# The first convolution pair: both column groups on each quarter of the tokens, and a first half loaded as two quarters

## The chip, the cores and the metric

The kernel is one program on one core of a Trainium2 chip. The metric is the device time of that core in microseconds (us), the median of the runs. On this kernel a difference of about 0.2%, some 3.8 us, is what a measurement can tell from no change.

## What is computed

One layer of a hybrid decoder. Tokens are 16 meta tokens, 256 prompt tokens and 8 sequences of 8 new tokens, 336 in all, each with 2048 features. Cut to the lines that concern the start:

```python
xn = rmsnorm(x, g_mix)                       # 336 tokens x 2048
z = xn @ w_in + b_in
zq, zk, zv, zi, zf, zo, zu, zc, zb, zga, zgb = jnp.split(z, _split_points(), axis=-1)
...
conv_out, conv_state = conv_fn(zc * zu, w_conv)   # 1024 channels, 3 taps, causal
y_b = zb * conv_out
```

All is in float32. The mLSTM heads, the gated merge and the squared-ReLU MLP follow and are not touched by the change.

## The kernel before

**Products and units.** Every float32 operand is split into a high and a low part, and a product is three matmuls (high by high, high by low, low by high; line 1250 issues each). The weights come in units of 512 rows by 256 columns (512 KB). One unit is 24 matmuls: 4 blocks of 128 rows, 2 blocks of 128 columns, 3 products. A unit passes through a ring of four slots on its way: SP loads it into `raw` (L378), ACT copies its high part (`w_high`, L543), DVE subtracts to get its low part (`w_low`, L823), and PE multiplies. Semaphores tie the four: SP refills a slot once its low part is made, ACT and DVE write a slot's parts once PE has used the unit that was in it. So each engine works through the units in one fixed order, written out in its own program.

**The start.** The tokens arrive token by token in `x_tok`, in two halves of 1024 feature columns: five DMAs each, on SP's queue (`tokens`, L364 to L373). PE transposes them, two blocks of 128 columns at a time (six transposes, L1270), into one of two pairs of PSUM banks, `XBANKS`. From there ACT makes `x_high` (L561), scaled by a column of `vec_T`, DVE makes `x_low` (L840) and a plain copy `x_T` (L843). `vec_T` itself comes from four small DMAs on ACT's queue (`vec_rows`), a transpose on PE (L1258) and a copy on DVE (L816). ACT also sums the squares of the tokens (L551), from which DVE and ACT make the norm's factors; PE spreads them over the partitions (`scales`, `r_diag`), and DVE copies the result to `r_bc` (L871).

**The first convolution pair.** For 256 channels, the columns of zu and then those of zc are computed, four units each: numbered here 0 to 3 (zu, accumulated in `ACC[0]`) and 4 to 7 (zc, `ACC[1]`). The first units are interleaved with the transposes: unit 0 needs the first quarter of the features, and so on. DVE takes each group out of PSUM and multiplies it by `r_bc` (`tmp`, L900), ACT adds the bias (L588, L594), and DVE multiplies zu by zc and runs the three taps (L904 to L925). The other three pairs follow, units 8 to 15 being the second; two of the pairs are a loop. On ACT and DVE a unit's split stands ahead of its use by three (`LEAD`), so before the taps of pair 0 DVE has made the low parts through unit 10.

Of the kernel before, what the change touches and what calls it, by code (L numbers as in the profile page):

```python
# [29 lines left out]
P = 128  # L30
# [13 lines left out]
def build(nc, x_prompt, x_sample, state_C, state_n, state_m, state_conv, meta, g_mix, w_in, b_in,  # L44
# [65 lines left out]
    with ExitStack() as ctx:  # L110
# [121 lines left out]
        HEAD_ACC = [0, 1, 0, 1, 2]  # L232
        XBANKS = [ACC[1], ACC[2]]

# [13 lines left out]
        s_brows = sem("bias_rows_in")  # L248
        s_xtok = [sem(f"x_tok_in{n}") for n in range(6)]
        s_gw = sem("gate_w_in")  # L250
# [112 lines left out]
        def _(sp):  # L363
            def tokens(half):  # L364

                c = slice(D // 2 * half, D // 2 * half + D // 2)
                in0, in1, in2 = s_xtok[3 * half:3 * half + 3]
# [12 lines left out]

            def convolution(i, extra=()):
                for g, col in enumerate((CU, CC)):
                    for u in range(NU):
                        if NU * g + u in extra:
                            extra[NU * g + u]()
                        stream(UCV * i, NU * g + u, win, u, col + GC * i)

            def small():
# [139 lines left out]
        def _(act):  # L528
# [16 lines left out]
            def sum_squares(half, n):  # L545

                nt, done = (P, P, NMETA + TS)[n], 3 * half + n
                act.wait_ge(s_xtok[done], 16 if n == 1 else 32)
# [24 lines left out]
            def gate_weights():  # L573
# [4 lines left out]
                a.activation(gws[:, :, 32:32 + H], gw[:, :, H:2 * H], ACT.Copy).then_inc(s_ghl, 1)  # L578

            def convolution(i, extra=()):  # L580
                for p in range(UCV):
                    split(UCV * i, p + LEAD)
                    if p in extra:
                        extra[p]()
                    if p == 3:
                        act.wait_ge(evacuated, 2 + 2 * i + 1)
                        for b in range(GB):
                            ins = a.activation(zu[:, b, :], tmp[:, b, 0:TZ], ACT.Identity,  # L588
                                               bias=biasT[:, ds(BU + GB * i + b, 1)])
                        ins.then_inc(s_zu, 1)  # L590
                    if p == 7:
                        act.wait_ge(evacuated, 2 + 2 * i + 2)
                        for b in range(GB):
                            ins = a.activation(tmp[:, b, 0:TZ], tmp[:, b, 0:TZ], ACT.Identity,  # L594
                                               bias=biasT[:, ds(BC_ + GB * i + b, 1)])
                        ins.then_inc(s_zc, 1)

# [15 lines left out]

            convolution(0, {1: root, 2: gate_weights, 3: lambda: act.wait_ge(s_col, 2)})
            with act.Fori(1, H - 1) as i:
# [192 lines left out]
        def _(dve):  # L808
# [29 lines left out]
            for k in range(KB):  # L838
# [3 lines left out]
                if k % 2 == 1:  # L842
                    v.tensor_copy(xT[:, k - 1:k + 1, T0:T], XBANKS[k // 2 % 2][:, :, T0:T]).then_inc(s_xT, 1)  # L843
                if k % 4 == 3 and k // 4 < LEAD:
                    split(0, k // 4)

# [38 lines left out]
            scale_o = rbc[:, T0:T].unsqueeze(1).to_broadcast([P, GB, TO])  # L885

            def convolution(i, extra=()):
                for p in range(UCV):
# [3 lines left out]
                    if p in (3, 7):  # L892
                        g = p // 4
                        dve.wait_ge(unit_used, RING + UCV * i + 4 * g + 4)
                        if g == 0:
                            dve.wait_ge(s_z, 1 + i)
                            dve.wait_ge(s_cv, 1 + 12 * i)
                        else:
                            dve.wait_ge(s_zu, i + 1)
                        v.tensor_tensor(tmp[:, :, 0:TZ], ACC[g][:, :, 0:TZ], scale_z, ALU.mult).then_inc(evacuated, 1)  # L900
                    if p == 7:

                        dve.wait_ge(s_zc, i + 1)
                        v.tensor_copy(zs[:, :, :, 0:TAPS - 1], stT[:, ds(GB * i, GB), :, :])  # L904
                        v.tensor_tensor(zp[:], tmp[:, :, 0:ZP], zu[:, :, 0:ZP], ALU.mult)
                        v.tensor_tensor(zs[:, :, :, TAPS - 1:], tmp[:, :, ZP:TZ].rearrange("p g (b t) -> p g b t", t=DS),
                                        zu[:, :, ZP:TZ].rearrange("p g (b t) -> p g b t", t=DS), ALU.mult) \
                            .then_inc(s_z, 1)
                        dve.wait_ge(s_z, 1 + i + 1)
                        v.tensor_copy(zlast[:, ds(GB * i, GB), 0:TAPS - 1], zp[:, :, ZP - TAPS + 1:ZP])  # L910
                        v.tensor_copy(zlast[:, ds(GB * i, GB), TAPS - 1:].rearrange("p g (b r) -> p g b r", r=TAPS - 1),
                                      zs[:, :, :, DS:DS + TAPS - 1])

                        for r in range(TAPS):
                            for b in range(GB):
                                w = vecT[:, ds(VC + r * (CW // P) + GB * i + b, 1)]
                                out_p = yb[:, ds(GB * i + b, 1), 0:SEQ]
                                out_s = yb[:, ds(GB * i + b, 1), SEQ:TO].rearrange("p o (b t) -> p (o b) t", t=DS)
                                src_p = zp[:, b:b + 1, r:r + SEQ]
                                src_s = zs[:, b, :, r:r + DS]  # L920
                                for out, src in ((out_p, src_p), (out_s, src_s)):
                                    if r == 0:
                                        v.tensor_scalar(out, src, w, None, ALU.mult).then_inc(s_cv, 1)
                                    else:
                                        v.scalar_tensor_tensor(out, src, w, out, ALU.mult, ALU.add).then_inc(s_cv, 1)  # L925
                            dve.wait_ge(s_cv, 1 + 12 * i + 4 * r + 4)


# [53 lines left out]

            convolution(0, {1: columns, 3: scales, 5: gate_weights})
            with dve.Fori(1, H - 1) as i:
# [263 lines left out]
        def _(pe):  # L1248
# [11 lines left out]
            def tokens(k):  # L1260

                for n in range(3):
                    pe.wait_ge(s_xtok[3 * (k // (KB // 4)) + n], 16 if n == 1 else 32)
                if k >= 2:
# [48 lines left out]

            def convolution(i, extra=()):
                for p in range(UCV):
                    if p in extra:
                        for work in extra[p]:
                            work()
# [4 lines left out]
            def four_blocks(u):  # L1323

                return [lambda: tokens(2 * u), lambda: tokens(2 * u + 1), lambda: pe.wait_ge(s_xl, UK * u)]

            tokens(0)
            tokens(1)
            convolution(0, {0: four_blocks(1), 1: four_blocks(2), 2: four_blocks(3) + [columns],
                            3: [lambda: pe.wait_ge(s_xl, KB)], 4: [scales]})  # L1330
            with pe.Fori(1, H - 1) as i:
# [230 lines left out]
```

## Time and the profile before

| | |
|---|---|
| runs | 1911.57 us median of 3 (1911.06 to 1912.3) |
| profiled execution, first to last instruction | 1911.0 us |
| PE busy | 1889.9 us (99%) |
| DVE busy, ACT busy | 941.6 us (49%), 689.5 us (36%) |

The page gives no time of the profiled execution but its span; the median of the runs is 0.57 us above it. PE is busy nearly all the time, so what can be gained or lost is time in which PE waits, or runs at its low clock.

### The profile page before, as it was taken

To read this page: it belongs to the slowest core of one execution; us is meant where nothing else is said; L and a number is where in the kernel's file an instruction comes from. 1 tells how busy PE (TensorE), PEld (TensorE's weight loads), DVE (VectorE), ACT (ScalarE), POOL (GpSimd) and SP (SyncE) were. 2 spreads that over 40 slices of the span, in tenths; PEclk is the share of its full clock that TensorE was granted. 3 is DMA by queue.
4 is the path that set the end of the run, shared out by engine and by line. 5 is a ranking of instruction groups with operands and counts; after the bars stand their busy time and mean duration, and the time that the engine had idled before them with its cause. 6 is when DMAs were issued, how large, how long until landed. Compare 5 with 4: busy or idle time off the path is not lost.

```text
span 1911.0 us, 33610 instructions
## 1 busy us (share of the span) xinstructions
PE 1889.9 (99%) x12647; PEld 1855.8 (97%) x12647; DVE 941.6 (49%) x1045; ACT 689.5 (36%) x825; POOL 34.5 (2%) x67
## 2 busy tenths in 40 slices
PE   7999999999999999999999999999999999999998
PEld 7999898989899999999999999999999999999997
DVE  6565545454454444445555544455444544455544
ACT  5344343434343333333443333333333333333331
POOL 1001000010100000000000000000000000000000
PEclk9999999999999999999999999999999999999998
DMA  7446564756465545544454444444444444444442
GB/s 208 144 127 190 132 213 133 220 119 216 138 177 146 151 143 155 152 148 148 143 172 156 140 159 145 151 150 141 160 145 151 150 147 154 143 154 151 145 155 78
DMA packets 294469, 293.86 MB, mean 154 GB/s; under 512 B 12506, under 2 KB 292314, under 8 KB 294300
## 3 DMA queue, kind: packets, MB, share of 16 engines
q1 hardware_dynamic: 283464, 282.67, 48.8%
q10 hardware_dynamic: 10692, 9.51, 1.6%
q0 software_dynamic: 272, 1.12, 0.1%
q8 instruction: 27, 0.44, 0.1%
q14 instruction: 14, 0.11, 0.0%
HBM read 281.10 MB, written 12.17 MB: 153 GB/s over the span
## 4 chain that ended last, share of the span: by engine, by line
PE 98%; DVE 1%; DMA 0%; issue 0%; ACT 0%; SPq 0%; DVEq 0%; ACTq 0%
PE ps L1250 97%; DVE y_out L1243 0%; PE ps L1350 0%; DMA x_tok<-in_x_sample_dram 0%; PE ps L1270 0%; DVE x_low L840 0%; DVE x_T L843 0%; PE ps L1507 0%; DVE w_low L823 0%; ACT x_high L561 0%; PE ps L1451 0%; DVE sq_acc L1216 0%; DVE x_T L1212 0%; ACT tmp L790 0%; DVEq L110 0%
## 5 line engine op out<-in xcount | busy, mean ns | idle before, releaser
L823 DVE TENSOR_TENSOR w_low<-raw,w_high 128x1024 fp32r<-128x1024 f32 x512 | 621.7, 1226 | 609.0 <-ACT w_high L543 605.1
L543 ACT ACTIVATE w_high<-raw 128x1024 fp32r<-128x1024 f32 x512 | 534.9, 1055 | 712.5 <-PE ps L1250 709.1
L1250 PE MATMUL ps<-x_high,w_high 128*128 128x320 f32 (+2 forms) x2432 | 755.5, 311 | 1.3 <-PE ps L1250 1.1
L1250 PE MATMUL ps<-x_low,w_high 128*128 128x320 f32 (+2 forms) x2432 | 755.8, 311 | 0.0
L1250 PE MATMUL ps<-x_high,w_low 128*128 128x320 f32 (+2 forms) x2432 | 753.2, 310 | 0.0
L1250 PEld LDWEIGHTS ps<-x_high,w_high 128*128 128x128 f32 x2432 | 457.5, 188 | 7.2 <-issue 4.6
L1250 PEld LDWEIGHTS ps<-x_high,w_low 128*128 128x128 f32 x2432 | 458.6, 189 | 0.0
L1250 PEld LDWEIGHTS ps<-x_low,w_high 128*128 128x128 f32 x2432 | 457.3, 188 | 0.1
L1250 PE MATMUL ps<-u_high,w_high 128*128 128x320 f32 x1024 | 316.5, 309 | 0.0
L1250 PE MATMUL ps<-u_low,w_high 128*128 128x320 f32 x1024 | 316.4, 309 | 0.0
L1250 PE MATMUL ps<-u_high,w_low 128*128 128x320 f32 x1024 | 316.4, 309 | 0.0
L1250 PEld LDWEIGHTS ps<-u_high,w_high 128*128 128x128 f32 x1024 | 192.2, 188 | 0.0
L1250 PEld LDWEIGHTS ps<-u_low,w_high 128*128 128x128 f32 x1024 | 192.2, 188 | 0.0
L1250 PEld LDWEIGHTS ps<-u_high,w_low 128*128 128x128 f32 x1024 | 192.2, 188 | 0.0
L1250 PE MATMUL ps<-merged_high,w_high 128*128 128x320 f32 x256 | 79.1, 309 | 0.0
L1250 PE MATMUL ps<-merged_low,w_high 128*128 128x320 f32 x256 | 79.1, 309 | 0.0
L1250 PE MATMUL ps<-merged_high,w_low 128*128 128x320 f32 x256 | 79.1, 309 | 0.0
L774 ACT ACTIVATE u_high<-u_squared 128x640 f32 (+1 forms) x32 | 23.7, 739 | 140.2 <-DVE u_squared L1191 140.2
L1212 DVE TENSOR_TENSOR x_T<-ps,x_T 128x640 f32 (+1 forms) x32 | 26.4, 825 | 54.1 <-PE ps L1250 54.1
L1250 PEld LDWEIGHTS ps<-merged_high,w_high 128*128 128x128 f32 x256 | 48.0, 188 | 0.0
L1250 PEld LDWEIGHTS ps<-merged_low,w_high 128*128 128x128 f32 x256 | 48.0, 188 | 0.0
L1250 PEld LDWEIGHTS ps<-merged_high,w_low 128*128 128x128 f32 x256 | 48.0, 188 | 0.0
(250 smaller groups left out, 1160.2 us busy)
## 6 DMA issues: line engine op xcount, KB each, us to landing
raw<-in_w_in_dram SPq DMA_DIRECT2D x176, 512.0 KB, 3.8
raw<-in_w_up_dram SPq DMA_DIRECT2D x128, 512.0 KB, 3.9
raw<-in_w_down_dram SPq DMA_DIRECT2D x128, 512.0 KB, 3.4
raw<-in_w_o_dram SPq DMA_DIRECT2D x32, 512.0 KB, 3.5
C_state<-in_state_mlstm_C_dram SPq DMA_DIRECT2D x16, 512.0 KB, 6.5
raw<-in_state_mlstm_C_dram SPq DMA_DIRECT2D x16, 512.0 KB, 4.1
out_dram<-C_state ACTq DMA_DIRECT2D x8, 1024.0 KB, 6.8
raw<-in_p_a_dram SPq DMA_DIRECT2D x16, 512.0 KB, 4.3
```

Source lines behind the costliest of these rows:

```text
L543: a.activation(wh[:, s % RING], raw[:, s % RING], ACT.Copy).then_inc(high_done, 1)
L774: a.activation(uh[:, ds(GB * j, GB), :], uq[:], ACT.Copy).then_inc(s_uh, 1)
L823: v.tensor_tensor(wl[:, s % RING], raw[:, s % RING], wh[:, s % RING].bitcast(F32), ALU.subtract).then_inc(low_done, 1)
L1212: v.tensor_tensor(x2, ACC[pair][:, :, 0:TO], x2, ALU.add).then_inc(evacuated, 1)
L1250: return pe.matmul(out, lhsT, rhs, start=start, stop=stop)
```

## The change

Three things, all ahead of the second pair. The first half of the tokens' columns comes as two quarters, so there are three parts (`XPARTS`) and fifteen DMAs in place of ten. The first pair's units go by quarter: unit numbers 0, 2, 4, 6 are zu and 1, 3, 5, 7 are zc, and the two that share a quarter follow each other. And the bank pair `ACC[1]`, which now holds zc from the start, is no longer used for transposes; banks 4 and 5 are, where `vec_rows` and the other small rows are transposed too, so PE waits for DVE's copy of `vec_T` before the first token transposes. The later steps of the first pair are written out again for each engine.

The parts, and SP's order of issue (`tokens` takes the part's number, `first_convolution` replaces the first call of the loop's body):

```diff
-        XBANKS = [ACC[1], ACC[2]]
+        XBANKS = [ps[:, 4:6, :], ACC[2]]
+        XPARTS = [(0, D // 4), (D // 4, D // 2), (D // 2, D)]
...
+            def first_convolution(extra):
+                for u in range(NU):
+                    for g, col in enumerate((CU, CC)):
+                        stream(0, 2 * u + g, win, u, col)
+                        if 2 * u + g in extra:
+                            extra[2 * u + g]()
...
             tokens(0)
-            convolution(0, {1: lambda: tokens(1), 3: small, 4: gates})
+            first_convolution({1: lambda: tokens(1), 2: lambda: tokens(2), 3: small, 4: gates})
```

ACT, from the first tokens to the end of the first pair:

```diff
             act.wait_ge(s_set, 1)
-            for n in range(2):
-                sum_squares(0, n)
             act.wait_ge(s_col, 1)
             for k in range(KB):
...
-                if k % 4 == 3 and k // 4 < LEAD:
-                    split(0, k // 4)
-                    if k < 4:
-                        sum_squares(0, 2)
-                    sum_squares(1, k // 4)
+                if k % UK == UK - 1:
+                    u = k // UK
+                    split(0, 2 * u)
+                    split(0, 2 * u + 1)
+                    if u > 0:
+                        for done in (2 * u - 2, 2 * u - 1):
+                            sum_squares(done // 3, done % 3)
...
+            def first_convolution():
+                root()
+                gate_weights()
+                split(0, UCV)
+                act.wait_ge(s_col, 2)
+                bias_u(0)
+                split(0, UCV + 1)
+                bias_c(0)
+                split(0, UCV + 2)
```

DVE behind the splits of the first pair, and PE:

```diff
+            def first_convolution():
+                columns()
+                gate_weights()
+                scales()
+                split(0, UCV)
+                evacuate_z(0, 0, UCV - 1)
+                split(0, UCV + 1)
+                evacuate_z(0, 1, UCV)
+                split(0, UCV + 2)
+                convolve(0)
...
+            def first_convolution():
+                pe.wait_ge(s_col, 1)
+                tokens(0)
+                tokens(1)
+                for u in range(NU):
+                    if u < NU - 1:
+                        tokens(2 * u + 2)
+                        tokens(2 * u + 3)
+                    pe.wait_ge(s_xl, UK * (u + 1))
+                    for g in range(2):
+                        if (u, g) == (NU - 1, 0):
+                            pe.wait_ge(s_xT, KB // 2)
+                            columns()
+                        if (u, g) == (NU - 1, 1):
+                            scales()
+                        if u == 0:
+                            pe.wait_ge(evacuated, g + 1)
+                        unit(0, 2 * u + g, ACC[g][:, :, 0:TZ], xh, xl, UK * u, TZ0, u == 0, u == NU - 1)
```

`evacuate_z`, `convolve`, `bias_u` and `bias_c` are the bodies that stood in the loop before, unchanged. On SP, `gates` (the gate weights' DMA and three tiny ones) now stands behind the load of unit 4 instead of ahead of it.

How the order moves, at three places. ACT at the very start, before (`y_b` is scratch space for the squares, `x_tok_in0` is the landing of the first half's first rows):

```order
L551 ACT_TABLE_LOAD [waits x_tok_in0]
L551 ACTIVATE y_b,sum_sq_halves<-x_tok 128x1024 [waits columns_set]
L551 ACTIVATE y_b,sum_sq_halves<-x_tok 128x1024 [waits sum_sq_ready,x_tok_in1]
L561 ACTIVATE x_high<-ps,vec_T 128x336 [waits x_transposed,cols_ready]
L561 ACTIVATE x_high<-ps,vec_T 128x336 [waits x_transposed] x3
L543 ACTIVATE w_high<-raw 128x1024 [waits unit_used,raw_landed0]
```

and after, the same place:

```order
L567 ACT_TABLE_LOAD [waits x_transposed,cols_ready]
L567 ACTIVATE x_high<-ps,vec_T 128x336 [waits columns_set]
L567 ACTIVATE x_high<-ps,vec_T 128x336 [waits x_transposed] x3
L551 ACTIVATE w_high<-raw 128x1024 [waits unit_used,raw_landed0]
L551 ACTIVATE w_high<-raw 128x1024 [waits unit_used,raw_landed1]
L567 ACTIVATE x_high<-ps,vec_T 128x336 [waits x_transposed] x4
```

The two sums of squares that stood ahead of `x_high` are gone from there, so the load of ACT's function table, which stands ahead of the first activation, now waits for the first transposes (`x_transposed`) and not for the first tokens. Two weight splits follow where one did.

DVE around the end of the first pair, before (`raw_landed` 3, 0, 1, 2 mark the low parts of units 7, 8, 9 and 10; `tmp` is the evacuation of zu, then of zc; `z_sample` begins the product and the taps):

```order
L871 COPY r_bc<-ps 128x336 [waits r_bc_product]
L900 TENSOR_TENSOR tmp<-ps,r_bc 128x2x322 [waits z_ready,conv_step,unit_used,r_bc_ready]
L823 TENSOR_TENSOR w_low<-raw,w_high 128x1024 [waits unit_used,raw_landed3,high_done]
L823 TENSOR_TENSOR w_low<-raw,w_high 128x1024 [waits unit_used,raw_landed0,high_done]
L878 TENSOR_TENSOR gate_w_split<-gate_w,gate_w_split 128x16x4 [waits gate_w_split,gate_w_in]
L880 TENSOR_TENSOR gate_w_split<-gate_w,gate_w_split 128x16x4
L823 TENSOR_TENSOR w_low<-raw,w_high 128x1024 [waits unit_used,raw_landed1,high_done]
L823 TENSOR_TENSOR w_low<-raw,w_high 128x1024 [waits unit_used,raw_landed2,high_done]
L900 TENSOR_TENSOR tmp<-ps,r_bc 128x2x322 [waits zu_ready,unit_used]
L904 COPY z_sample<-conv_state_T 128x16x2 [waits zc_ready]
```

and after (`raw_landed` 0, 1, 2 are units 8, 9 and 10):

```order
L896 COPY r_bc<-ps 128x336 [waits r_bc_product]
L847 TENSOR_TENSOR w_low<-raw,w_high 128x1024 [waits raw_landed0,unit_used,high_done,r_bc_ready]
L919 TENSOR_TENSOR tmp<-ps,r_bc 128x2x322 [waits conv_step,z_ready,unit_used]
L847 TENSOR_TENSOR w_low<-raw,w_high 128x1024 [waits unit_used,raw_landed1,high_done]
L919 TENSOR_TENSOR tmp<-ps,r_bc 128x2x322 [waits zu_ready,unit_used]
L847 TENSOR_TENSOR w_low<-raw,w_high 128x1024 [waits unit_used,raw_landed2,high_done]
L923 COPY z_sample<-conv_state_T 128x16x2 [waits zc_ready]
L924 TENSOR_TENSOR z_prompt<-tmp,zu 128x516
```

Both evacuations now stand between the copy of `r_bc` and the taps, with the low parts of units 8, 9 and 10 put between them one by one. In both kernels the low part of unit 11 is DVE's next piece of work behind the taps.

ACT at the same place, before (`gate_w_split` ends the gate weights; `zu` and `tmp` are the two biases; `raw_landed` 2, 3, 0, 1, 2 are the high parts of units 6 to 10):

```order
L543 ACTIVATE w_high<-raw 128x1024 [waits unit_used,raw_landed2]
L588 ACTIVATE zu<-tmp,bias_T 128x322 [waits evacuated,cols_ready]
L588 ACTIVATE zu<-tmp,bias_T 128x322
L543 ACTIVATE w_high<-raw 128x1024 [waits unit_used,raw_landed3]
L543 ACTIVATE w_high<-raw 128x1024 [waits unit_used,raw_landed0]
L543 ACTIVATE w_high<-raw 128x1024 [waits unit_used,raw_landed1]
L543 ACTIVATE w_high<-raw 128x1024 [waits unit_used,raw_landed2]
L594 ACTIVATE tmp<-tmp,bias_T 128x322 [waits evacuated]
L594 ACTIVATE tmp<-tmp,bias_T 128x322
```

and after (units 8, 9 and 10):

```order
L551 ACTIVATE w_high<-raw 128x1024 [waits unit_used,raw_landed0]
L591 ACTIVATE zu<-tmp,bias_T 128x322 [waits evacuated,cols_ready]
L591 ACTIVATE zu<-tmp,bias_T 128x322
L551 ACTIVATE w_high<-raw 128x1024 [waits unit_used,raw_landed1]
L598 ACTIVATE tmp<-tmp,bias_T 128x322 [waits evacuated]
L598 ACTIVATE tmp<-tmp,bias_T 128x322
L551 ACTIVATE w_high<-raw 128x1024 [waits unit_used,raw_landed2]
```

The high parts of units 9 and 10 now each stand behind a bias, and each bias waits for an evacuation by DVE (`evacuated`).

## Rows read from the trace of the kernel before

**Rows 1.** Page, parts 1 and 6: engines' share; a weight unit's transfer, median to landing.
```profile
PE 1889.9 (99%) x12647; PEld 1855.8 (97%) x12647; DVE 941.6 (49%) x1045; ACT 689.5 (36%) x825; POOL 34.5 (2%) x67
...
raw<-in_w_in_dram SPq DMA_DIRECT2D x176, 512.0 KB, 3.8
```

**Rows 2.** Chain that ended last, in order of time: start us, us, what.
```profile
2.68 6.62 DMA x_tok<-in_x_sample_dram
...
16.41 5.31 PE ps L1250 x24
...
36.22 93.85 PE ps L1250 x631
```

**Rows 3.** Timeline of PE: start us, us, what, idle before and its releaser.
```profile
8.18 0.35 PE L1258 MATMUL ps<-ident,vec_rows 72*128 72x72 f32 x1 [8.18 <-DMA vec_rows<-in_w_conv_dram]
9.44 2.47 PE L1270 MATMUL ps<-ident,x_tok 128*128 128x128 f32 x12 [0.90 <-DMA x_tok<-in_x_sample_dram]
13.38 1.35 PE L1270 MATMUL ps<-ident,x_tok 128*128 128x128 f32 x6 [1.47 <-DVE x_T L843]
...
32.42 0.39 PE L1250 MATMUL ps<-x_high,w_high 128*128 128x322 f32 x1 [0.20 <-DVE w_low L823]
...
36.22 0.89 PE L1250 MATMUL ps<-r_diag,ones 128*128 128x128 f32 x6
36.91 0.39 PE L1250 MATMUL ps<-x_high,w_high 128*128 128x322 f32 x1
```

**Rows 4.** Timeline of ACT over the start, its DMA issues included.
```profile
2.48 0.65 ACTq L538 DMA_DIRECT2D vec_rows<-in_w_conv_dram  x1
5.42 1.28 ACT L551 ACT_TABLE_LOAD   x1 [5.42 <-DMA x_tok<-in_x_prompt_dram]
...
10.89 2.03 ACT L561 ACTIVATE x_high<-ps,vec_T 128x336 fp32r<-128x336 f32 x4 [1.78 <-PE ps L1270]
...
39.81 1.02 ACT L588 ACTIVATE zu<-tmp,bias_T 128x322 f32<-128x322 f32 x2 [3.21 <-DVE tmp L900]
...
52.29 1.02 ACT L594 ACTIVATE tmp<-tmp,bias_T 128x322 f32<-128x322 f32 x2 [3.30 <-DVE tmp L900]
53.21 1.05 ACT L543 ACTIVATE w_high<-raw 128x1024 fp32r<-128x1024 f32 x1
```

**Rows 5.** Timeline of DVE over the start.
```profile
8.57 0.23 DVE L816 COPY vec_T<-ps 128x72 f32<-128x72 f32 x1 [6.32 <-PE ps L1258]
...
38.35 0.50 DVE L871 COPY r_bc<-ps 128x336 f32<-128x336 f32 x1
38.88 0.83 DVE L900 TENSOR_TENSOR tmp<-ps,r_bc 128x644 f32<-128x644 f32 x1
41.81 2.36 DVE L823 TENSOR_TENSOR w_low<-raw,w_high 128x1024 fp32r<-128x1024 f32 x2 [2.10 <-ACT w_high L543]
...
53.34 0.18 DVE L904 COPY z_sample<-conv_state_T 128x32 f32<-128x32 f32 x1 [1.09 <-ACT tmp L594]
...
58.47 3.50 DVE L823 TENSOR_TENSOR w_low<-raw,w_high 128x1024 fp32r<-128x1024 f32 x3 [0.40 <-DVE y_b L925]
```

**Rows 6.** Timeline of SP's queue, 0 to 110 us.
```profile
13.66 7.17 SPq L397 DMA_DIRECT2D ig_bias<-in_b_in_dram  x1
```

**Rows 7.** The x_tok issue of 4.53 us alone: instruction, then issue to landing.
```profile
L369 SPq DMA_DIRECT2D x_tok<-in_x_prompt_dram x1: 449/449/449, 4.5 to 4.5; - x1
...
DMA to landing us min/median/max: 8.4/8.4/8.4
```

**Rows 8.** The raw issue of 8.21 us alone: instruction, then issue to landing.
```profile
L378 SPq DMA_DIRECT2D raw<-in_w_in_dram x1: 680/680/680, 8.2 to 8.2; - x1
...
DMA to landing us min/median/max: 11.1/11.1/11.1
```

**Rows 9.** Timeline of PE at the end of the program.
```profile
1897.19 1.18 PE L1250 MATMUL ps<-ones,sq_acc 128*128 128x1 f32 x6 [2.20 <-DVE sq_acc L1230]
```

**Rows 10.** Windows at the end: stretch, busy time (PE first), granted clock, DMA share, GB/s.
```profile
1897.40:1904.20 6.80, 6.37 (x31) 5.41 (x31) 5.35 (x14) 0.20 (x1) 0.00 (x0) 0.50 0.42 137
```

More of the change, by code:

```diff
@@ L248, in build @@
         s_brows = sem("bias_rows_in")
-        s_xtok = [sem(f"x_tok_in{n}") for n in range(6)]
+        s_xtok = [sem(f"x_tok_in{n}") for n in range(3 * len(XPARTS))]
         s_gw = sem("gate_w_in")
@@ L363, in _, with tokens @@
         def _(sp):
-            def tokens(half):
-                c = slice(D // 2 * half, D // 2 * half + D // 2)
-                in0, in1, in2 = s_xtok[3 * half:3 * half + 3]
+            def tokens(part):
+                c = slice(*XPARTS[part])
+                in0, in1, in2 = s_xtok[3 * part:3 * part + 3]
                 sp.dma_start(xtok[0:NMETA, 0, c], meta[:, c]).then_inc(in0, 16)
@@ L547, in sum_squares @@
                 nt, done = (P, P, NMETA + TS)[n], 3 * half + n
-                act.wait_ge(s_xtok[done], 16 if n == 1 else 32)
+                for part in ((0, 1), (2,))[half]:
+                    act.wait_ge(s_xtok[3 * part + n], 16 if n == 1 else 32)
                 if done > 0:
@@ L578, in gate_weights, with bias_u, bias_c @@
                 a.activation(gws[:, :, 32:32 + H], gw[:, :, H:2 * H], ACT.Copy).then_inc(s_ghl, 1)
+            def bias_u(i):
+                act.wait_ge(evacuated, 2 + 2 * i + 1)
+                for b in range(GB):
+                    ins = a.activation(zu[:, b, :], tmp[:, b, 0:TZ], ACT.Identity,
+                                       bias=biasT[:, ds(BU + GB * i + b, 1)])
+                ins.then_inc(s_zu, 1)
+            def bias_c(i):
+                act.wait_ge(evacuated, 2 + 2 * i + 2)
+                for b in range(GB):
+                    ins = a.activation(tmp[:, b, 0:TZ], tmp[:, b, 0:TZ], ACT.Identity,
+                                       bias=biasT[:, ds(BC_ + GB * i + b, 1)])
+                ins.then_inc(s_zc, 1)
             def convolution(i, extra=()):
@@ L585, in convolution @@
                     if p == 3:
[L586 to L590, printed above, removed]
-                    if p == 7:
[L592 to L596, printed above, removed]
+                        bias_u(i)
+                    if p == 7:
+                        bias_c(i)
+            def first_convolution():
[7 more added lines that the diff above has]
+                split(0, UCV + 2)
             def log1p_exp():
@@ L843, in _ @@
                     v.tensor_copy(xT[:, k - 1:k + 1, T0:T], XBANKS[k // 2 % 2][:, :, T0:T]).then_inc(s_xT, 1)
-                if k % 4 == 3 and k // 4 < LEAD:
-                    split(0, k // 4)
+                if k % UK == UK - 1:
+                    split(0, 2 * (k // UK))
+                    split(0, 2 * (k // UK) + 1)
             def columns():
@@ L892, in convolution @@
                     if p in (3, 7):
[L893 to L900, printed above, removed]
@@ L901, in convolution @@
-                    if p == 7:
[L903 to L926, printed above, removed]
@@ L929, in _ @@
+                        evacuate_z(i, p // 4, p + 1)
+                    if p == 7:
+                        convolve(i)
+            def first_convolution():
[8 more added lines that the diff above has]
+                convolve(0)
             step = [0]
@@ L981, in decays @@
                                   [:, :, DS - 1]))
-            convolution(0, {1: columns, 3: scales, 5: gate_weights})
+            first_convolution()
             with dve.Fori(1, H - 1) as i:
@@ L1260, in tokens @@
             def tokens(k):
+                part = next(i for i, (c0, c1) in enumerate(XPARTS) if c0 <= 2 * P * k < c1)
                 for n in range(3):
-                    pe.wait_ge(s_xtok[3 * (k // (KB // 4)) + n], 16 if n == 1 else 32)
+                    pe.wait_ge(s_xtok[3 * part + n], 16 if n == 1 else 32)
                 if k >= 2:
@@ L1312, in unit, with convolution @@
                 ins.then_inc(unit_used, 1)
-            def convolution(i, extra=()):
+            def convolution(i):
                 for p in range(UCV):
-                    if p in extra:
-                        for work in extra[p]:
-                            work()
                     if p % 4 == 0:
@@ L1321, in convolution @@
                     unit(UCV * i, p, ACC[p // 4][:, :, 0:TZ], xh, xl, UK * (p % 4), TZ0, p % 4 == 0, p % 4 == 3)
[L1323 to L1330, printed above, removed]
+            def first_convolution():
[16 more added lines that the diff above has]
+                        unit(0, 2 * u + g, ACC[g][:, :, 0:TZ], xh, xl, UK * u, TZ0, u == 0, u == NU - 1)
+            first_convolution()
             with pe.Fori(1, H - 1) as i:
```

38 lines of the change are left out of this document (34 added, 4 removed).

## The prediction

> **What bounds the kernel now.** I read the page's first part first. PE is busy 99% of the span [rows 1], so a change to the start can only move the time by what it does to PE's waits and to PE's clock. Then I read the chain that ended last, in order of time: until 9.30 us it is the last tokens of the first half that land, then it goes over PE, ACT and DVE to the first unit at 16.41, and from 36.22 on PE alone carries it [rows 2]. So two things count: when unit 0 starts, and whether PE waits anywhere after it. PE's timeline shows the only such wait of the stretch, 0.20 us at unit 3 for a low part [rows 3]. A unit at full speed takes 24 matmuls at 93.85 / 631 = 0.149 us, 3.57 us; the first one takes 5.31 [rows 2], so it runs mostly at the low level of the clock and loses 1.74 us to it.
>
> The profiled execution has 1911.0 us from first to last instruction. The sum below is made against that; the runs' median lies 0.57 us above it, and I carry that over.
>
> **The start, up to unit 0.** The matmuls, transposes and splits are the same in number before and after; only order and transfers change.
>
> Less data before the first transposes. The first half is 336 rows of 4 KB, 1.38 MB, and its last piece lands at 2.68 + 6.62 = 9.30 [rows 2]. Its first two pieces (0.52 MB) had landed by 5.42, when ACT's wait for them ended [rows 4]. A first quarter has 0.69 MB. Between these two points that gives 6.2 us.
>
> `vec_rows`, which PE now also has to wait for, landed at 8.18 [rows 3]. Its last issue, at 2.48 [rows 4], stands between the pieces of the first half, and it landed before the piece issued at 2.68 did; transfers of the two queues seem to be served nearly in order of issue. With half the bytes ahead of it, it would land near 5.7, by the same two points. I take that; if its delay does not depend on the bytes ahead, it stays 8.18. A page's rule that bears on this: the Trainium skill, "DMA: Bandwidth & Descriptors", section "Queues, rings and completion order", says that each DMA engine takes turns between the queues that have work, packet by packet. By that, too, shorter packets ahead would bring `vec_rows` sooner, by an amount I can't work out; no sum hangs on it. Behind its landing come the transpose and the copy (8.18 to 8.80 [rows 3, 5]) and some 0.15 us until PE goes on: the token transposes start at 6.5 (8.95 at the other bound) in place of 9.44.
>
> A new step on the path: the function table. Before, ACT loaded it at 5.42, 1.28 us [rows 4], while nothing waited. Now it stands behind the wait for the first transposes, so `x_high` starts 1.3 us later than its data allow. From the first transposes to `x_high` it was 10.89 - 9.44 = 1.45 [rows 3, 4]; now 2.75, so 9.25 in place of 10.89. From there to unit 0 it took 5.52 us, which would give 14.8.
>
> But unit 0 now stands behind the transposes of the second quarter. Ahead of that quarter's end on SP's queue are two quarters and two units, 2.42 MB. Before, the piece issued at 4.53 ended at the same sum of bytes (half, unit, and two pieces), and landed 8.4 us later, at 12.9 [rows 7]. So PE starts these twelve transposes at 13.1, takes 2.47 for them as for the first twelve [rows 3], and starts unit 0 at 15.57: 0.84 us earlier than 16.41. This landing, not the chain through ACT, is what sets it. If `vec_rows` stays at 8.18, the chain sets it: 8.95 + 2.75 + 5.52 = 17.2, 0.8 us later than before. If the landing comes 1.8 us sooner than I take it, the chain's 14.8 is the floor: 1.6 us earlier than before.
>
> **From unit 0 to unit 7.** The wait of 0.20 at unit 3 goes, since by then the low parts are well ahead. The third part of the tokens ends at 4.32 MB on the queue, which was the sum of bytes behind the unit issued at 8.21; that landed 11.1 us later, at 19.3 [rows 8]. PE asks for it after two units, at 15.57 + 5.31 + 3.57 = 24.4: hidden by 5 us. On SP the gate weights move behind unit 4's load, and five more issues of 0.45 to 0.65 us [rows 4, 7] go ahead of them. The issue behind the gate weights held SP from 13.66 for 7.17 us [rows 6]; now it holds back unit 5. It would begin near 17 and end near 24.5; a unit lands 3.8 us later [rows 1], 28.3. Split by ACT and DVE (1.05 and 1.22 us [rows 4, 5]), it is needed at 15.57 + 5.31 + 4 x 3.57 + 2 x 1.2 (two sets of twelve transposes, at half of 2.47) = 37.6. Hidden, by more than 6 us.
>
> The clock's loss I leave at 1.74 us. It could be between nothing and twice that (two units run back to back now), so from 1.7 less to 1.7 more.
>
> **Unit 11, the new wait.** This is where I expect most of it to be given back. Before, DVE had made the low parts of units 8, 9 and 10 ahead of the second evacuation, and the taps lay beside units 8 to 10: the low part of unit 11 was begun at 58.47 [rows 5] and done at 59.7, while PE reached unit 11 only at 36.91 + 7 x 3.57 = 61.9. Now all of it hangs in one chain on PE's products for `r_bc`, which stand between units 6 and 7. Let S be their start (36.22 before [rows 3]); unit 7 starts 0.69 later, as unit 4 did. In units of us after S:
> the products end at 0.89, DVE's copy to `r_bc` goes from 0.95 to 1.48 (38.35 to 38.88 [rows 5]), the low part of unit 8 to 2.62 (a step of 1.14 and 1.22 for one alone: two took 2.36, three 3.50 [rows 5]), the first evacuation to 3.45 (0.83), and ACT starts the bias at 3.55. From the bias to DVE's low part behind the next high part it took 41.81 - 39.81 = 2.00 [rows 4, 5]; so the low part of unit 9 starts at 5.55, the second evacuation runs from 6.69 to 7.52, the second bias starts at 7.56, and the high part of unit 10 ends 53.21 + 1.05 - 52.29 = 1.97 later, at 9.53 [rows 4]. Its low part goes to 10.69. Then come the product and the taps, 58.47 - 53.34 = 5.13 [rows 5], to 15.82, and unit 11's low part, 1.22 more, to 17.04; PE, some 0.15 behind it, goes on at 17.2.
> PE itself is through units 7 to 10 at 0.69 + 4 x 3.57 = 14.97. So it waits 2.2 us. Units 8, 9 and 10 are in time by 0.8 to 1.8 us (low parts at 2.6, 6.7 and 10.7 against 4.3, 7.8 and 11.4, so 0.7 for unit 10). Behind unit 11 the next three low parts follow at 1.14 each, faster than PE's 3.57, so no second wait. This chain does not depend on when the start is over. I give it 1.8 to 2.5; nothing in the rows lets it be a gain.
>
> **The sum.** -0.84 - 0.20 + 2.2 = +1.2 us: span 1912.2, median 1912.8.
>
> **The rivals.**
> (A) The wait at unit 11 does not come, because DVE's steps are shorter there than the rows say or the taps fit beside PE's work as before. For it: the room before was 2.1 us. Against: every step is a row. It gives -1.04, 1910.5.
> (B) The clock falls in that wait; the slower side. At the end of the program PE waited 2.20 us [rows 9], and the granted clock stood at 0.50, the 1.2 GHz level, for the 6.80 us behind it [rows 10]; PE did only transposes around there, which speaks against it here, where full matmuls stand on both sides. A low stretch costs half its length: as long as the first unit's, 1.7 us, 1914.5; as long as at the end, 3.4 us, 1916.2. It passes 0.2% (1915.4) when the stretch is over 5.2 us. The Trainium skill, "TensorE: Matmul & The Clock Gate", section "Why this matters for your kernels", warns of idle gaps between bursts of matmuls for the same reason; by its rule a gap this short would not do it.
> (C) `vec_rows` lands no earlier, and the table stands on the path: +0.8 in place of -0.84, so +2.8, 1914.4.
> (D) The change does more at the start than I give it: the second quarter lands early, unit 0 at 14.8: -0.4 in all, 1911.2.
> (E) A transfer comes late after all (unit 5 or the third part): some +3 to +5, 1914.6 to 1916.6.
>
> **How the numbers follow.** The likeliest, +1.2 (1912 to 1914 with its bounds), has 0.50; A 0.11, B 0.17, C 0.12, D 0.06, E 0.04. The time is that of the likeliest, 1912.8. A at the low end and all but the long form of B and E at the high end give 1910.3 to 1915.6. Under 0.2% in either direction lies nearly all of it: only B with a long low stretch, B with C, or E goes beyond 1915.4, 0.12 together; a gain of 3.8 us would need unit 0 to start near 12 us with no wait at unit 11, for which I leave 0.03. The rest, 0.85, is within 0.2%.
>
> **What would show it.** In PE's timeline after: token transposes from about 6.5, an idle stretch until about 13.1 that the tokens end, unit 0 near 15.6, no wait until one of about 2.2 us that DVE's `w_low` ends, just behind four units that follow the `r_diag` products. In ACT's: a table load behind the first transposes. Wrong would be: no such wait (A), a granted clock of 0.50 near 65 us (B), or `vec_rows` still landing at 8.2 (C).

## The result, and the profile after

The changed kernel takes 1916.26 us (median of 10 runs, 1913.24 to 1916.9), the kernel before 1911.58 on the same chip (10 runs, 1911.06 to 1912.5): 1.0022 times as long, with an interval of 1.0013 to 1.003. That is 4.7 us slower, and above the range of the prediction. The profiled execution after has a span of 1914.2 us, its own device time is 1915.98; in every run here the device time lies 1.7 to 1.8 above the span.

The chain that ended last, after (start us, us, what), against [rows 2]:

```profile
7.48 7.68 DMA x_tok<-in_x_sample_dram
15.35 2.47 PE ps L1310 x12
17.82 7.97 PE ps L1289 x48
...
26.96 7.16 PE ps L1289 x48
...
43.26 4.39 PE ps L1289 x30
48.41 0.94 issue
49.36 0.83 DVE tmp L919
51.29 0.96 ACT w_high L551
52.45 0.97 issue
53.42 0.83 DVE tmp L919
55.30 0.96 ACT w_high L551
56.28 1.23 DVE w_low L847
...
62.55 1.24 DVE w_low L847
63.83 81.51 PE ps L1289 x536
```

Two things are to be seen. Unit 0 now starts at 17.82, behind a transfer of tokens, where it started at 16.41. And the chain leaves PE a second time: from 47.65 to 63.83 it runs over DVE and ACT, by evacuation, high part, low part and the taps, and comes back to PE at unit 11.

PE's timeline after, the rows that answer to [rows 3] and [rows 9]:

```profile
6.02 0.35 PE L1297 MATMUL ps<-ident,vec_rows 72*128 72x72 f32 x1 [6.02 <-POOL sample_mask L497]
7.91 2.48 PE L1310 MATMUL ps<-ident,x_tok 128*128 128x128 f32 x12 [1.54 <-DMA x_tok<-in_x_sample_dram]
15.35 2.47 PE L1310 MATMUL ps<-ident,x_tok 128*128 128x128 f32 x12 [4.97 <-DMA x_tok<-in_x_sample_dram]
...
46.85 0.79 PE L1289 MATMUL ps<-r_diag,ones 128*128 128x128 f32 x6
...
63.83 0.63 PE L1289 MATMUL ps<-x_high,w_high 128*128 128x322 f32 x1 [1.93 <-DVE w_low L847]
...
1900.78 0.81 PE L1289 MATMUL ps<-ones,sq_acc 128*128 128x1 f32 x6 [2.20 <-DVE sq_acc L1269]
```

Three marks tell where the time went. Unit 8: before, it began four units behind 36.91, at 36.91 + 4 x 3.57 = 51.19; after, at 46.85 + 0.69 + 3.57 = 51.11 (the rows of its first matmuls read 51.22 and 51.06). So the whole start, with all that moved in it, is worth next to nothing. Unit 11: PE waits 1.93 us for DVE's low part, a wait that the kernel before did not have. And the program's last wait: 1897.19 before [rows 9], 1900.78 now, 3.59 later. All of the loss between these two marks arises at unit 11, and the wait is only about half of it. The windows behind the wait show the other half (columns as in [rows 10]):

```profile
63.86:67.28 3.42, 3.42 (x13) 3.42 (x14) 3.32 (x3) 0.00 (x0) 0.00 (x0) 0.50 0.60 179
67.28:71.28 4.00, 4.00 (x29) 4.00 (x29) 0.83 (x1) 0.88 (x2) 0.00 (x0) 1.00 1.02 327
```

PE is busy through both, but at a granted clock of 0.50, the 1.2 GHz level, for 3.42 us: 13 matmuls in the first window, 29 in the second, somewhat longer one. Half of 3.42 is lost, 1.71. The sum: -0.08 (51.11 - 51.19) + 1.93 + 1.71 = 3.56, against 3.59 measured. Counted from first matmul to first matmul it comes out the same: unit 8 begins 0.16 earlier, from there to unit 11 it takes 2.09 longer, and from unit 11 to unit 12 another 1.64.

DVE's timeline after, from the copy of `r_bc` to unit 11, against [rows 5]:

```profile
47.67 0.51 DVE L896 COPY r_bc<-ps 128x336 f32<-128x336 f32 x1 [1.26 <-PE ps L1289]
48.22 1.22 DVE L847 TENSOR_TENSOR w_low<-raw,w_high 128x1024 fp32r<-128x1024 f32 x1
49.36 0.82 DVE L919 TENSOR_TENSOR tmp<-ps,r_bc 128x644 f32<-128x644 f32 x1
52.28 1.23 DVE L847 TENSOR_TENSOR w_low<-raw,w_high 128x1024 fp32r<-128x1024 f32 x1 [2.10 <-ACT w_high L551]
53.42 0.82 DVE L919 TENSOR_TENSOR tmp<-ps,r_bc 128x644 f32<-128x644 f32 x1
56.28 1.23 DVE L847 TENSOR_TENSOR w_low<-raw,w_high 128x1024 fp32r<-128x1024 f32 x1 [2.04 <-ACT w_high L551]
...
62.55 4.63 DVE L847 TENSOR_TENSOR w_low<-raw,w_high 128x1024 fp32r<-128x1024 f32 x4 [0.40 <-DVE y_b L944]
```

DVE twice stands idle for 2 us for a high part that ACT made behind a bias: the low parts of units 9 and 10 are late by that, the taps behind them too, and with them unit 11.

ACT's start, against [rows 4], and SP's row that answers to [rows 6]:

```profile
9.37 1.28 ACT L567 ACT_TABLE_LOAD   x1 [9.37 <-PE ps L1310]
10.67 1.83 ACT L567 ACTIVATE x_high<-ps,vec_T 128x336 fp32r<-128x336 f32 x4
...
16.74 2.09 ACT L567 ACTIVATE x_high<-ps,vec_T 128x336 fp32r<-128x336 f32 x4 [2.35 <-PE ps L1310]
```

```profile
17.61 8.85 SPq L405 DMA_DIRECT2D ig_bias<-in_b_in_dram  x1
```

The table load stands where it was expected, but the `x_high` behind it, from 10.67, is not what PE waits for; PE waits for the second quarter until 15.35.

### The profile page after: what moved, and what is told of

It is laid out like the page before. It is cut to its first block, busy times and chain, and to the rows that moved or that the text cites. A ratio compares the mean times of both kernels' runs of the same rounds, so it can differ in the third digit from the quotient of the medians.

```text
span 1914.2 us, 33616 instructions
## 1 busy us (share of the span) xinstructions
PE 1888.7 (99%) x12647; PEld 1855.4 (97%) x12647; DVE 941.5 (49%) x1045; ACT 689.1 (36%) x825; POOL 34.5 (2%) x67
## 4 chain that ended last, share of the span: by engine, by line
PE 97%; DVE 1%; DMA 0%; SPq 0%; issue 0%; ACT 0%; DVEq 0%; ACTq 0%
PE ps L1289 97%; DMA x_tok<-in_x_sample_dram 0%; DVE y_out L1282 0%; PE ps L1400 0%; PE ps L1310 0%; DVE y_b L944 0%; DVE w_low L847 0%; ACT w_high L551 0%; DVE tmp L919 0%; SPq L372 0%; PE ps L1557 0%; SPq L373 0%; SPq L380 0%; SPq L370 0%; PE ps L1501 0%
```

## The experiments

Theory 1: the loss is the wait at unit 11 and the low clock behind it, some 3.6 us together. Theory 2: the loss comes from the late start, by the second quarter's landing. Each experiment gives its median, the median of the kernel before among the same runs, and the ratio with its interval.

**Units 8 to 10 split earlier** (the changed kernel with this alone: on ACT all three ahead of the biases, on DVE units 8 and 9 ahead of the scales and unit 10 ahead of the second evacuation):

```diff
 ACT first_convolution()
                 split(0, UCV)
+                split(0, UCV + 1)
+                split(0, UCV + 2)
                 act.wait_ge(s_col, 2)
                 bias_u(0)
-                split(0, UCV + 1)
                 bias_c(0)
-                split(0, UCV + 2)
 DVE first_convolution()
-                scales()
                 split(0, UCV)
-                evacuate_z(0, 0, UCV - 1)
                 split(0, UCV + 1)
-                evacuate_z(0, 1, UCV)
+                scales()
+                evacuate_z(0, 0, UCV - 1)
                 split(0, UCV + 2)
+                evacuate_z(0, 1, UCV)
                 convolve(0)
```

> The changed kernel, with the high and low parts of units 8, 9 and 10 made before the biases and the second evacuation, so that the taps end earlier. Theory 1 (the wait of 1.9 us at unit 11 and the low clock behind it cost it all): no wait of PE at unit 11, clock at full level there, 3.5 us less than the changed kernel, so about 1 us above the kernel before or level with it. Theory 2 (the later start of unit 0 costs it): the wait goes, but the time stays at 4 to 5 us above the kernel before, less the 1.9 us of the wait, so +2.5 to +3.

Measured: 1912.56 against 1912.26, 1.0002 (0.9993 to 1.0011). PE's wait for the second quarter and its last wait, and a window over unit 11:

```profile
15.62 2.48 PE L1310 MATMUL ps<-ident,x_tok 128*128 128x128 f32 x12 [5.16 <-DMA x_tok<-in_x_sample_dram]
...
1897.14 0.81 PE L1289 MATMUL ps<-ones,sq_acc 128*128 128x1 f32 x6 [2.20 <-DVE sq_acc L1269]
```

```profile
60.00:68.00 8.00, 8.00 (x56) 8.00 (x55) 3.96 (x4) 2.30 (x4) 0.00 (x0) 1.00 0.86 264
```

PE still waits for the tokens, as long as in the changed kernel and as late, so the late start is kept. But it is busy for all of the 8 us around unit 11, at full clock, the last wait ends at 1897.14 (1897.19 before, 1900.78 in the changed kernel), and the loss against the kernel before goes from 4.7 to 0.3 us. Theory 2 falls: with the late start alone there is no loss that can be told. The order of a few calls on two engines makes all of it, within what these medians tell.

**The first half in one piece again** (the changed kernel otherwise):

```diff
-        XPARTS = [(0, D // 4), (D // 4, D // 2), (D // 2, D)]
+        XPARTS = [(0, D // 2), (D // 2, D)]
...
-            first_convolution({1: lambda: tokens(1), 2: lambda: tokens(2), 3: small, 4: gates})
+            first_convolution({1: lambda: tokens(1), 3: small, 4: gates})
...
```

> The changed kernel, with the first half of the tokens' columns again in one piece; pair order and the end of the first pair as changed. Theory 1: unit 0 back to about 17.2 us or earlier (the table load still stands behind the first transposes), the wait at unit 11 stays, so the time stays within 1 us of the changed kernel. Theory 2 (the quarters' late landing is what costs): 1.5 us or more faster than the changed kernel.

Measured: 1916.44 against 1912.26, 1.0018 (1.0009 to 1.0027). ACT's timeline at its start, then PE's at unit 11 with the window behind it:

```profile
10.71 1.28 ACT L567 ACT_TABLE_LOAD   x1 [10.71 <-PE ps L1310]
```

```profile
64.18 0.41 PE L1289 MATMUL ps<-x_high,w_high 128*128 128x322 f32 x1 [1.93 <-DVE w_low L847]
```

```profile
65.01:68.42 3.41, 3.41 (x15) 3.41 (x14) 2.52 (x3) 0.00 (x0) 0.00 (x0) 0.50 0.87 229
```

Without quarters the wait, the low stretch and the time are the same, so the quarters are not what costs. Of the eleven runs six lie from 1916.44 to 1917.05 and five from 1913.76 to 1915.54: not every execution lost as much. The four lowest have a mean granted clock of 0.998 or 0.999, the other seven 0.996 or 0.997. This run doesn't test theory 2 by itself: its start is late too, for another reason, since the table load, with no later landing to hide it, here stands between the first transposes and `x_high`.

**The wait alone, put into the kernel before.** DVE makes n copies ahead of unit 11's low part; they write scratch space, and nothing else changes:

```diff
...
             convolution(0, {1: columns, 3: scales, 5: gate_weights})
+            for n in range(5):
+                v.tensor_copy(sqacc[:], xT[:, 0:GB, T0:T]).then_inc(s_pad, 1)
+                dve.wait_ge(s_pad, n + 1)
```

> The kernel before, with five copies of 0.84 us each put on DVE behind the taps of the first pair, ahead of the low part of unit 11 (their result is not used). Nothing else moves. The room there was 2.1 us, so PE waits about 2.1 us at unit 11. Theory 1 (a wait of this length also drops the clock): the granted clock stands at 0.50 behind the wait and the kernel is 3.5 to 4 us slower than before. Rival (the wait costs only itself): +2.1 us, clock unchanged.

Five copies were too few. I had priced them at 0.84 each, and they took 0.52 (DVE's timeline), so that PE waited only 0.34:

```profile
58.03 2.61 DVE L986 COPY sq_acc<-x_T 128x640 f32<-128x640 f32 x5
```

```profile
62.32 0.41 PE L1254 MATMUL ps<-x_high,w_high 128*128 128x322 f32 x1 [0.34 <-DVE w_low L824]
```

1912.68 against 1912.26, 1.0003 (0.9993 to 1.0012): this run decides nothing. With the copies' true price the count was set anew: seven, eight and twelve.

> The kernel before, with seven DVE copies ahead of unit 11's low part: a wait of 1.93 - 0.52 = 1.4 us there. If every wait beyond some tenths lowers the clock: +1.4 + 1.7 = +3.1, 1915.0, with 0.50 for 3.4 us behind it. If it takes a longer one: +1.4, 1913.3, at full clock.

> The kernel before, with eight DVE copies of 0.52 us each ahead of unit 11's low part (five gave a wait of 0.34 there). Both theories: three more copies make PE wait 0.34 + 3 x 0.52 = 1.9 us at unit 11. Theory 1 (the wait itself lowers the clock): granted clock 0.50 for about 3.4 us behind it, so +1.9 + 1.7 = +3.6 against the kernel before, 1915.8. Rival (the clock fell in the changed kernel for another reason, such as its later rise at the start): only the wait, +1.9, 1914.2, and no stretch at 0.50.

> The same with twelve copies: a wait of 0.34 + 7 x 0.52 = 4.0 us at unit 11. Theory 1: the clock falls too, in the short form (3.4 us at 0.50, +4.0 + 1.7 = +5.7, 1917.9) or in the long form seen behind the wait at the end of the program (6.8 us, +7.4, 1919.6). Rival: +4.0, 1916.2, at full clock.

PE's timeline at unit 11 for seven, eight and twelve copies:

```profile
62.66 0.41 PE L1254 MATMUL ps<-x_high,w_high 128*128 128x322 f32 x1 [1.40 <-DVE w_low L824]
```

```profile
64.28 0.41 PE L1254 MATMUL ps<-x_high,w_high 128*128 128x322 f32 x1 [1.93 <-DVE w_low L824]
```

```profile
66.41 0.64 PE L1254 MATMUL ps<-x_high,w_high 128*128 128x322 f32 x1 [4.04 <-DVE w_low L824]
```

And the windows behind these waits, in the same order:

```profile
62.66:66.00 3.34, 3.34 (x22) 3.34 (x23) 3.34 (x3) 0.00 (x0) 0.00 (x0) 1.00 0.59 173
```

```profile
64.91:68.32 3.41, 3.41 (x15) 3.41 (x14) 2.73 (x3) 0.00 (x0) 0.00 (x0) 0.50 0.75 210
```

```profile
65.09:71.91 6.82, 5.50 (x20) 5.50 (x21) 4.63 (x4) 0.00 (x0) 0.00 (x0) 0.50 0.60 176
```

| copies | PE's wait | clock behind it | median | against before | all runs |
|---|---|---|---|---|---|
| 7 | 1.40 | 1.00 | 1913.58 | +1.7, 1.0008 (0.9999 to 1.0017) | 1913.05 to 1914.12 |
| 8 | 1.93 | 0.50 for 3.41 us | 1915.94 | +4.1, 1.0017 (1.0008 to 1.0026) | five at 1913.28 to 1914.51, six at 1915.94 to 1917.31 |
| 12 | 4.04 | 0.50 for 6.82 us, 1.32 of it still in the wait | 1917.9 | +6.0, 1.0031 (1.0019 to 1.0044) | four at 1917.57 to 1918.05, two at 1919.47 and 1919.51 |

(The kernel before: 1911.87 beside the seven copies, 1911.89 beside the others.) Half a microsecond of DVE work between seven and eight copies costs 2.4 us of the median. With 1.40 us the wait costs about its own length. With 1.93 the runs part into two groups: the lower lies 2.0 above the kernel before, which is the wait alone, the upper, in which the profiled execution lies, 4.3 above it. The changed kernel's ten runs part in the same way: nine from 1915.89 to 1916.9, one at 1913.24; the mean granted clock of the nine is 0.996 or 0.997, that of the one 0.999 (with eight copies that number doesn't part the groups: 0.997 in the lower, 0.996 or 0.997 in the upper). Of the six runs with twelve copies, four fit the short low stretch that was expected (1917.9) and two the long one (1919.6); the profile is one of these two. So a wait as it stands in the changed kernel, in an otherwise untouched kernel, makes the same loss. What theory 1 would have put on the wait and the low stretch for the upper group is 1.93 + 1.71 = 3.6, 0.7 less than 4.3. In the profile it closes: with eight copies the last wait ends at 1901.21, 4.02 later than before, of which 0.30 was there ahead of unit 4 (the products for `r_bc` begin at 36.52, before at 36.22), so 3.7 arises behind it. The 0.7 is a matter of the medians and stays open. Ahead of unit 4 executions of this one start do differ by more than that: the products begin at 35.42, 36.14, 36.22, 36.52 and 36.53 in the profiles with seven, five, no, eight and twelve copies.

**Can the start be made to pay?** The changed kernel with units 8 to 10 ahead, both quarters issued ahead of any weights, and a tiny activation at ACT's start that brings the function table in while nothing waits:

```diff
+            a.activation(ssum[:], spart[:, 0], ACT.Square)
             act.wait_ge(s_col, 1)
...
             tokens(0)
-            first_convolution({1: lambda: tokens(1), 2: lambda: tokens(2), 3: small, 4: gates})
+            tokens(1)
+            first_convolution({1: lambda: tokens(2), 3: small, 4: gates})
...
```

> The changed kernel with three things at once: the splits of units 8 to 10 ahead as in the first kernel of this call; both quarters issued ahead of the first two units' loads; and a tiny activation at ACT's start so that the function table is loaded early. If the second quarter's landing behind two units is what holds unit 0 back: unit 0 near 15 us, no wait at unit 11, 1 to 2.5 us faster than the kernel before. If the DMA queue is simply slower with 2 KB rows: unit 0 near 16.5, level with the kernel before.

Then the same with the first half in one piece:

> The changed kernel with its first half in one piece, the splits of units 8 to 10 ahead of the scales and biases, and a tiny activation that brings ACT's function table in early. If the table stood on the path to unit 0 (it did in the version with one piece, where unit 0 began at 17.3), unit 0 begins 1.3 us earlier, near 16.0, with no wait at unit 11: 1911 or a little less, equal to the kernel before. If transfers set the start all the same, unit 0 stays at 17.3. Since an earlier start lies mostly in the low stretch of the clock, at most half of it is kept: 1910.5 to 1912.

Measured: 1910.79 against 1912.26, 0.9993 (0.9984 to 1.0002), and 1911.44 against 1911.89, 0.9997 (0.9988 to 1.0006). Both are much better than the changed kernel, and neither is told from the kernel before. The chains of the two, the first with both quarters, the second with one half:

```profile
12.63 1.07 ACT w_high L552
13.72 1.24 DVE w_low L849
15.09 10.04 PE ps L1291 x48
25.13 1.17 PE ps L1312 x12
```

```profile
2.68 7.39 DMA x_tok<-in_x_sample_dram
...
17.19 8.71 PE ps L1290 x48
25.90 1.17 PE ps L1311 x12
```

With both quarters ahead, tokens no longer hold unit 0; its own weights do (DMA, high part, low part). Now read units 0 and 1 of the three kernels side by side: begun at 15.09, 17.19 and 17.82, they take 10.04, 8.71 and 7.97 us and end at 25.13, 25.90 and 25.79. A start 2.7 us earlier ends 0.7 earlier. PE's matmuls follow each other at 0.27 us until the clock has risen and at 0.15 behind that. This turn came at 21.1, 20.6 and 19.6 us in the three profiles, latest where unit 0 began first. So two things took the gain. At one and the same turn 0.15 / 0.27 of the 2.7 would be left, about 1.5 (an estimate from the two spacings); the turn that came 1.5 us later costs some 0.7 of that. The turn also moves between executions of one start, from 18.6 to 20.7 us in the five profiles of the kernel before and its versions with copies, so 0.7 is what was left in one execution and not a price.

The version with one half did not begin unit 0 near 16.0, as it was to if the table load had been all that held it: the load was off the path, but the half landed at 10.07, where it landed at 8.88 in the version with one half above, which began unit 0 at 17.53.

**What made the second quarter late?** Two variants of the transfers in the kernel before: the first half's five transfers cut by rows into nine (the largest into four of 32 rows), and five transfers with two pieces of 2 KB a row (the features then stand in another order, and the output is that of the reordered tokens).

```diff
...
-                sp.dma_start(xtok[:, 1, c], x_prompt[0, P - NMETA:2 * P - NMETA, c]).then_inc(in1, 16)
+                rows(1, 0, x_prompt[0], P - NMETA, in1)
...
```

```diff
...
-                sp.dma_start(xtok[:, 1, c], x_prompt[0, P - NMETA:2 * P - NMETA, c]).then_inc(in1, 16)
+                sp.dma_start(dst(0, P, 1), src(x_prompt[0, P - NMETA:2 * P - NMETA, :])).then_inc(in1, 16)
...
```

> The kernel before, with the first half's five token transfers cut by rows into nine, the rows 4 KB as before: the same bytes in more transfers. Two quarters ahead of the units landed at 10.43 where the half in five transfers landed at 9.30. If the number of transfers costs that, the half lands near 10.3 here; if the shorter rows (2 KB) do, it stays at 9.3.

> The kernel before, its tokens in ten transfers as before, but each of them takes the features in two pieces of 2 KB a row in place of one of 4 KB (first quarters 0 and 2, then 1 and 3; the features thereby stand in another order in the tokens, and the output is that of the reordered tokens). If 2 KB rows are what made the quarters slow, the half lands near 10.4 and unit 0's weights near 12.3, as in the version with both quarters ahead (12.6); if the number of transfers did it, they land where the kernel before had them, 9.3 and 11.2, give or take 0.6.

PE's first token transposes, which wait for the half, with nine transfers and with 2 KB rows:

```profile
10.46 2.47 PE L1278 MATMUL ps<-ident,x_tok 128*128 128x128 f32 x12 [2.82 <-DMA x_tok<-in_x_sample_dram]
```

```profile
10.77 2.48 PE L1276 MATMUL ps<-ident,x_tok 128*128 128x128 f32 x12 [2.29 <-DMA x_tok<-in_x_sample_dram]
```

Both are later than the 9.44 of [rows 3]; but in the version above with one half, five transfers and 4 KB rows, the same place reads 10.21 (2.68 + 7.39 = 10.07 for the landing). The landing of one and the same half varies by 1.2 us between kernels (8.88 in the first version with one half, 9.30 before, 10.07 here), so neither variant tells transfers from row length, and each was run once; whether either costs anything is not shown. What is shown is only the place in the queue: issued ahead of two units the second quarter landed at 10.4 (issued 5.39, 5.0 to landing), behind them at 15.16.

## Why the prediction was wrong

**The failed step is "The clock's loss I leave at 1.74 us", with rival B held for unlikely (0.17).** The prediction had the wait at unit 11 right, in place, cause and size (2.2 forecast, 1.93 measured), but took it at its own length. Behind the wait the granted clock stood at 0.50 for 3.42 us, which is B in its short form, +1.7. The seven and eight copies show that this belongs to the wait and not to anything else in the change. I had weighed against B that at the end of the program PE did only transposes around its wait, and that here full matmuls stand on both sides. For the side ahead of the wait that was misread. PE's timeline before has:

```profile
1893.81 0.31 PE L1250 MATMUL ps<-u_high,w_low 128*128 128x320 f32 x1
1893.96 1.03 PE L1507 MATMUL ps<-ident,x_T 128*128 128x128 f32 x8
```

Full matmuls run up to 1893.96, then come eight transposes of 1.03 us in all, and then the wait of 2.20 [rows 9]. The nearest row spoke for B more than against it, and that full matmuls on both sides do not protect the clock is what the runs show. The Trainium skill, "TensorE: Matmul & The Clock Gate", section "Why this matters for your kernels", warns of gaps longer than this one, and I used it against B. Here the measurement decides: 1.93 us was followed by the low level in most executions, and with 1.40 none of the eleven run times shows a fall.

**The second quarter's landing was mis-sized.** I took 12.9 from a transfer with equal bytes ahead of it; it landed 2.3 later, at 15.16, and unit 0 began at 17.82 in place of 15.57, that is 1.41 later than before and not 0.84 earlier. Equal bytes on the queue did not mean an equal landing: the first quarter too landed at 7.8 and not at 6.2. Two differences that the sum left out show in the traces. The piece that ends the second quarter is the twelfth issue on SP, at 7.48, where the piece that I took its landing from was the eighth, at 4.53. And between 5 and 6 us the DMA engines moved 97 GB/s at a share of 0.47, where before they moved 218 at 0.98. Which of these made it late is not shown. The form of the step was right, the tokens and not the table load set unit 0, and the floor that the chain through ACT gives was not reached.

**Two errors at the start cancelled.** The later start cost little because the loss to the clock, which I had left alone, shrank with it: units 0 and 1 took 7.97 us in place of 5.31 + 3.57 = 8.88, and the wait of 0.20 at unit 3 went as forecast. That is 1.11 of the 1.41. The rest lies at unit 3 as well, which ran slower behind its wait (the chain before):

```profile
32.42 3.78 PE ps L1250 x24
```

Units 2 and 3 took 7.81 before, from 28.41 to the products for `r_bc` at 36.22; they take 7.16 now. The 0.91 of units 0 and 1 and these 0.65 make 1.56, which is the 1.41 and the 0.16 by which unit 8 begins earlier. So the start came out at -0.1 where the sum had -1.04. That the two errors met so nearly is luck.

**What held.** `vec_rows` came early with less data ahead of it: 5.7 was forecast for the landing, and its transpose ran at 6.02, put down to GpSimd (POOL) and not to a transfer, so the landing was no later than that. So rival C fell. The table load moved behind the first transposes and was hidden; with one half, where that cover is gone, it stood on the path as costed. The third part was due at 25.6 and landed at 23.5 (issued 10.68, 12.8 to landing; 19.3 forecast), so its cover was 2 us and not 5, but it held. The gate weights held SP for 8.85 us from 17.61, and PE did not notice. Rivals A and D did not come, and neither of the two transfers of E stalled PE; the one that did was the second quarter.

**The size.** By the two profiled executions the forecast of +1.2 stands against +3.59 at the program's last wait: +0.94 from the start (-0.1 for -1.04), -0.27 from the wait, +1.71 from the clock make 2.4 of difference, which closes. From that wait to the end of the span it is 13.8 us before and 13.4 after, where the low stretch is 3.41 us long (1903.65 to 1907.06) and not 6.80 [rows 10], so the two spans differ by 3.2. The medians are 4.68 apart, 1.5 more. The execution of the kernel before that I read had a span of 1911.0, so a device time near 1912.8 and 1.2 above its median; the profiled one after is 0.3 below its own. A prediction that adds its sum to the median isn't moved by that, but the terms read between these two profiles add up to 1.5 less than the medians' difference. Where the 1.5 lie in the runs that were not profiled stays open; the profiles show executions of one start up to 1.1 apart ahead of unit 4, and some 0.4 apart behind the last wait. With B's short form alone the forecast would have been 1914.5, within its range; the start's 0.94 and these 1.5 carried the time past it.

## What to carry to other kernels

When a reordering leaves the matmul engine a new wait, price the wait twice: at its length, and at its length plus half of a low stretch of the clock, and look for the next-longer wait in the trace that was followed by one. Look first at what stands behind a wait on the helping engines: here a few calls in another order, with no work added, were the difference between 4.7 us above the kernel before and 0.3. Ask also which execution a profile shows: one of these was 1.2 us above its kernel's median, as much as the whole forecast. And a start that lies within the clock's first low stretch is worth a fraction of its microseconds: of 2.7 us gained at unit 0, 0.7 were left two units later, in one execution of each kernel.

## What was unexpected of the hardware

A wait of 1.93 us between dense matmuls was followed by a stretch at 0.50 in the three kernels whose profile shows such a wait (3.41 or 3.42 us each), and the same kernels' runs lie up to 3 us apart in a way that fits a fall in most and none in the others (in two of the three kernels as two clear groups); 1.40 us was followed by none. With twelve copies the clock fell while PE still waited, 1.32 us before the wait of 4.04 ended. In the first units the matmuls' pitch of 0.27 us shows the low level, though the windows' column of the granted clock reads 1.00 there (before, 16 matmuls in the 3.80 us from 16.20), as it does ahead of the first recorded change; the pitch is what tells. And an SBUF copy of 128 x 640 float32 on DVE took 0.52 us, where the evacuation of 128 x 644 that I had priced it by takes 0.82.
